# An encoder layer with a routed mixture of experts: the experts' token columns selected on TensorE instead of passing through DRAM, and the norms between the stages moved off GpSimd

## The chip, the core and the metric

One NeuronCore of a Trainium2 chip runs the whole program. The metric is the device time of one execution in microseconds (us). TensorE is called PE here, its weight load PEld, VectorE DVE, ScalarE ACT, GpSimd POOL and SyncE SP. PE's granted clock has two levels in the profile, 1.2 and 2.4 GHz (0.50 and 1.00).

## What is computed

One encoder layer on two requests of 256 tokens (512 tokens, width 1024, all fp32). The first part is a token mixer (a wide input projection, spatial gating, multi-scale pooling, an output projection). The part that matters here comes after it:

```
x = LN(alpha * x + gate1 * t) * ln1_g + ln1_b          # t: the mixer's output
h = LN(x) * (1 + scale2) + shift2                       # h2 in the kernel
# router: top-1 group of 4, then top-2 of the 8 experts in the group, per token
out[token] += weight * (silu(h @ w_gate[e]) * (h @ w_up[e])) @ w_down[e]   # 32 experts, hidden 512
y = LN(alpha * x + gate2 * out) * ln2_g + ln2_b
```

Each token goes to two experts, so 1024 rows are spread over 32 experts, 32 on the mean. An expert is worked in rounds of CAP = 64 rows; one that has more gets further rounds. With these inputs one expert has a further round.

## The kernel before, in words

Every engine's instructions stand in one written order, with semaphores between the engines. The program has three stages.

The mixer (span 0 to 439.5 us) ends with the projection by w_out: eight halves (4 tiles of 128 tokens, 2 halves of 512 columns), each 24 matmuls of 128x512. DVE multiplies a half by gate1 out of PSUM (L1644), POOL adds it to the residual (L583, `half_out`).

The transition makes x and h2 of each of the 4 tiles. DVE computes both norms with bn_stats and bn_aggr (L1638, L1656, L1661, L1667, L1674, L1710), ACT takes the roots (L1247, L1251), DVE inverts them with a Newton step of five small operations. h2 is then written chunk by chunk: `by_chunk` on ACT (L1255) reads `scaled` in steps of 8 elements and writes h2 as [token, 8 chunks, 128], POOL adds shift2 (L588, `shifted`). For the last tile DVE does both in two operations (L1728). PE transposes h2 of each tile (L876) and multiplies by the router's weights (L684, `wr`), tile after tile, with dummy transposes (`keep_clock`, L881) behind. DVE makes the routing decisions from the logits (L1751 to L1788). PE counts rows per expert with small bf16 matmuls. DVE makes each assignment's row number (`pos`, L1801) and POOL scatters h2's rows, sorted by expert, into the DRAM tensor `packed_x` with 8 indirect DMAs (L608). For the first expert alone the rows are selected on PE from h2, with one-hot columns `sel` as the stationary side and h2 as the moving side, and transposed (L1029 to L1035).

The expert stage (482.6 to 969.7 us) runs the experts one after another. The 6 MB of weights of one expert, gate_w, up_w and down_w, are loaded by SP into three sets of buffers, `next_expert`: gate and up for expert e when expert e-3's are read, down when expert e-3's is read. Ahead of them SP loads the expert's 64 rows from `packed_x` into `xrows` (`load_rows`, L426). On PE an expert is: 32 matmuls of 64 stationary and 512 moving columns for gate and up (two column halves of the array work side by side), 4 transposes of the next expert's rows (L926), 4 transposes of the hidden values (L942), 16 matmuls for down. DVE and ACT make the steps between: silu (L1297), the product (L1888), `x_t` of the next expert (L1849), the columns of hid (L1072), the gated output (L1906). POOL stores the output rows to DRAM (L615), and each token gathers its two rows at the end.

An fp32 matmul is two rows for PE in the trace (hi and lo), an fp32 transpose is one. In the listings the weight-load side of a form is what stands first (128*64 is 128 partitions and 64 stationary columns), the moving side second.

```
def x_transposes(rows, bank, s):              # L926, before: 4 transposes per expert
    for k in range(KC // 2):
        x = pe.transpose(bank[:, cols], rows[:, cols], ident)
def h_transposes(hd, bank, sm):               # L942, before and after: 4 per expert
    view = hd[:, :].rearrange("c (p f) -> c f p", f=FC)       # FC = 4: steps of 16 bytes
```

Of the kernel before, what the change touches and what calls it, by code (L numbers as in the profile page):

```python
# [5 lines left out]
D = 1024  # L6
REQ = 2
SEQ = 256
TOK = REQ * SEQ
KC = D // 128  # L10
TILES = TOK // 128
HALF = 64
# [27 lines left out]
def hybrid_encoder(nc, x_prompt, x_sample, c_prompt, c_sample, w_mod, b_mod, w_in, b_in, w_spatial,  # L40
# [7 lines left out]
    packed_x = nc.dram_tensor("packed_x", (ASSIGN + 8 * CAP, D), f32).ap()  # L48
    mod_rows_d = nc.dram_tensor("mod_rows_d", (2, REQ, 2, 512), f32).ap()
    shift2_d = nc.dram_tensor("shift2_d", (REQ, KC, 2, 64), f32).ap()  # L50
# [3 lines left out]
    with ctx:  # L54
# [38 lines left out]
        halves = [at(f"half{i}", [128, 512], f32, SLOT + (32 + 2 * i) * K) for i in range(3)]  # L93
        scaled = [at(f"scaled{i}", [128, D], f32, SLOT + (38 + 4 * i) * K) for i in range(2)]
        last_half = at("last_half", [128, 512], f32, SLOT + 46 * K)
        gate1_bc = at("gate1_bc", [128, D], f32, S0 + 9728 + 8192)
        shift2_bc = at("shift2_bc", [128, KC, 128], f32, 2 * SLOT + 40 * K)
# [6 lines left out]
        is_last = at("is_last", [128, 2, TILES, CAP], f32, 2 * SLOT + 40 * K)  # L104
        scaling = at("scaling", [128, 2, 2, 128], f32, 2 * SLOT + 40 * K)
        weighed = at("weighed", [128, 2, TILES, CAP], f32, 2 * SLOT + 42 * K)
# [23 lines left out]
        pos = at("pos", [128, 2, TILES], u32, S0 + 2464)  # L130
        pos_y = at("pos_y", [128, 2, TILES], u32, S0 + 2496)
        tab = at("tab", [1, 5, NEXP + 1], i32, S0 + 2528)
# [5 lines left out]
        rel_last = at("rel_last", [128, 2, TILES], f32, P0 + 288)  # L138
        slot_p = at("slot_p", [128, 1], f32, S0 + 3392)
        assert P0 + 320 + base <= nc.sbuf_usable_end  # L140
        gate2_half = [at(f"gate2_half{r}", [128, 512], f32, o) for r, o in enumerate((T0 + 6144, S0 + 7680))]
        slot_gate = at("slot_gate", [128, 512], f32, T0 + 10240)
        slot_gate_x = at("slot_gate_x", [128, 512], f32, T0 + 27648)
        n0_next = at("n0_next", [128, NEXP], f32, T0 + 25600)
        slots_last = at("slots_last", [128, CAP], f32, T0 + 25728)
# [14 lines left out]
        h2 = [at(f"h2_{i}", [128, KC, 128], f32, T0 + o) for i, o in enumerate((12288, 16384, 20480, 8192))]  # L160
# [6 lines left out]
        onehot = at("onehot", [128, 2, TILES, NEXP], f32, Q0 + 736)  # L167
# [8 lines left out]
        slots = at("slots", [128, CAP], f32, T0 + 2176)  # L176
        sel = at("sel", [128, 2, TILES, CAP], f32, T0 + 2432)
        before_m = at("before_m", [128, 4, 128], bf16, T0 + 512)
        request_m = at("request_m", [128, 2, 128], bf16, T0 + 5504)
        slot_tmp = at("slot_tmp", [128, 2, CAP], f32, T0 + 2432)  # L180
        assert Q0 + 3936 + base <= nc.sbuf_usable_end

        xrows = [at(f"xrows{i}", [128, 512], f32, T0 + 4096 * i) for i in range(3)]

        x_t = [at(f"x_t{i}", [128, KC, CAP], f32, T0 + o) for i, o in enumerate((29696, 14336, 16384))]
        sg = at("sg", [CAP, DE], f32, T0 + 18432)
        hid = at("hid", [CAP, DE], f32, T0 + 20480)
        hid_t = at("hid_t", [128, FC, CAP], f32, T0 + 22528)
        yout = [at(f"yout{i}", [128, 512], f32, o) for i, o in enumerate((T0 + 23552, S0 + 3584, S0 + 5632))]
        xrows_x = at("xrows_x", [128, 512], f32, T0 + 2048)  # L190
        x_first = at("x_first", [CAP, D], f32, T0 + 25600)
        x_t_x = at("x_t_x", [128, KC, CAP], f32, T0 + 12288)
        sg_x = at("sg_x", [CAP, DE], f32, T0 + 31744)
        hid_x = at("hid_x", [CAP, DE], f32, T0 + 33792)
        hid_t_x = at("hid_t_x", [128, FC, CAP], f32, T0 + 35840)
        yout_x = at("yout_x", [128, 512], f32, T0 + 36864)
# [29 lines left out]
        s_wr = sem("s_wr")  # L226
        s_ln2 = sem("s_ln2")
        s_zero = sem("s_zero")
        s_scat = sem("s_scat")
        s_out = sem("s_out")  # L230

        pe_pro = sem("pe_pro")
# [137 lines left out]
        def _(sp):  # L370
# [88 lines left out]
            for e in range(3):  # L459
                load_rows(e, offset(e))  # L460
# [1611 lines left out]
```

## Time and profile before

| what | value |
|---|---|
| time before, median of 3 runs | 1003.95 us (1002.37 to 1005.49) |
| the profiled execution | 1002.76 us, span 1001.2 us, so 1.6 us lie outside the span |
| PE busy | 874.3 us, 87% of the span |
| DVE, ACT, POOL busy | 379.3, 209.4, 141.8 us |
| DMA | 310.50 MB, mean 310 GB/s |
| mean granted PE clock | 0.957 |

The page cuts the span in 40 slices of 25 us. A digit is a busy share in tenths. The windows view gives the same for stretches that one chooses: busy time and count for each engine, then the mean granted clock, the share of the DMA engines and GB/s. The timeline lists instructions in order of time, runs of equal ones merged into one row with their count; its second number is then the time from the start of the first to the end of the last. In the views by tile a row gives shortest, median and longest duration in ns.

### The profile page before, as it was taken

To read this page: it belongs to the slowest core of one execution; us is meant where nothing else is said; L and a number is where in the kernel's file an instruction comes from. 1 tells how busy PE (TensorE), PEld (TensorE's weight loads), DVE (VectorE), ACT (ScalarE), POOL (GpSimd) and SP (SyncE) were. 2 spreads that over 40 slices of the span, in tenths; PEclk is the share of its full clock that TensorE was granted. 3 is DMA by queue.
4 is the path that set the end of the run, shared out by engine and by line. 5 is a ranking of instruction groups with operands and counts; after the bars stand their busy time and mean duration, and the time that the engine had idled before them with its cause. 6 is when DMAs were issued, how large, how long until landed. Compare 5 with 4: busy or idle time off the path is not lost.

```text
span 1001.2 us, 12712 instructions
## 1 busy us (share of the span) xinstructions
PE 874.3 (87%) x4001; PEld 502.7 (50%) x4002; DVE 379.3 (38%) x672; ACT 209.4 (21%) x302; POOL 141.8 (14%) x192
## 2 busy tenths in 40 slices
PE   3789999999999999969778888997868888887895
PEld 2457677888888887859323233332223233322231
DVE  4522443565343247896412222222122122212145
ACT  2321334441234244122300000000000000000024
POOL 2210267000001000340300000000000000000041
PEclk9799999999999999986999999999999999999998
DMA  9894653365647624449699999999999999999984
GB/s 366 325 299 172 218 206 138 115 236 187 236 181 192 206 86 149 146 158 426 224 419 424 426 426 428 427 426 427 427 428 427 427 427 425 431 425 429 422 337 133
DMA packets 52557, 310.50 MB, mean 310 GB/s; under 512 B 5058, under 2 KB 7202, under 8 KB 36898
## 3 DMA queue, kind: packets, MB, share of 16 engines
q1 hardware_dynamic: 41104, 272.64, 67.2%
q0 software_dynamic: 10800, 35.64, 10.4%
q10 hardware_dynamic: 610, 1.66, 0.6%
q8 instruction: 26, 0.43, 0.2%
q14 instruction: 17, 0.14, 0.0%
HBM read 284.46 MB, written 25.45 MB: 310 GB/s over the span
## 4 chain that ended last, share of the span: by engine, by line
PE 60%; DMA 22%; DVE 6%; issue 3%; SPq 3%; ACT 3%; POOL 1%; DVEq 0%; POOLq 0%; ACTq 0%
PE bank L684 58%; DMA up_w<-in_w_exp_up 18%; DMA modraw<-in_w_mod 2%; SPq L385 2%; PE bank L942 1%; DVE hid L1888 1%; ACT sg L1297 1%; DVE res L1661 1%; DMA y_first<-round_y,pos_y 1%; DMA packed_x<-h,pos 1%; ACT hid_t L1072 1%; PE bank L881 1%; PE bank L876 1%; POOL packed_x L608 1%; DMA round_y<-yout 0%
## 5 line engine op out<-in xcount | busy, mean ns | idle before, releaser
L684 PE MATMUL bank<-gate_w,x_t 128*64 128x512 f32 x512 | 234.2, 611 | 28.7 <-DMA up_w<-in_w_exp_up 20.6
L684 PE MATMUL bank<-up_w,x_t 128*64 128x512 f32 x512 | 234.3, 612 | 0.0
L684 PEld LDWEIGHTS bank<-gate_w,x_t 128*64 128x64 f32 x512 | 70.6, 141 | 183.4 <-issue 180.0
L684 PE MATMUL bank<-down_w,hid_t 128*64 128x512 f32 x496 | 121.7, 636 | 14.7 <-ACT hid_t L1072 14.7
L684 PE MATMUL bank<-h_hi,w_hi 128*128 128x512 f32 x320 | 126.5, 395 | 1.6 <-ACT h_hi L1106 1.6
L684 PE MATMUL bank<-h_hi,w_lo 128*128 128x512 f32 x320 | 126.3, 395 | 0.0
L684 PE MATMUL bank<-h_lo,w_hi 128*128 128x512 f32 x320 | 125.0, 398 | 0.0
L1888 DVE TENSOR_TENSOR hid<-bank,sg 64x512 f32<-64x512 f32 x31 | 21.5, 693 | 226.7 <-ACT sg L1297 226.7
L1437 DVE TENSOR_TENSOR w_lo<-raw,w_hi 128x1024 fp32r<-128x1024 f32 x56 | 68.6, 1227 | 78.6 <-ACT w_hi L1072 78.5
L1297 ACT ACTIVATE sg<-bank 64x512 f32<-64x512 f32 x31 | 18.3, 590 | 378.8 <-PE bank L684 378.8
L615 POOL DMA_DIRECT2D round_y<-yout x31 | 16.1, 519 | 423.3 <-issue 423.3
L684 PEld LDWEIGHTS bank<-down_w,hid_t 128*64 128x64 f32 x496 | 34.8, 144 | 78.6 <-issue 59.6
L684 PEld LDWEIGHTS bank<-h_lo,w_hi 128*128 128x128 f32 x320 | 60.3, 189 | 25.1 <-issue 11.6
L684 PEld LDWEIGHTS bank<-up_w,x_t 128*64 128x64 f32 x512 | 70.5, 141 | 0.0
L1072 ACT ACTIVATE w_hi<-raw 128x1024 fp32r<-128x1024 f32 x56 | 58.9, 1053 | 53.3 <-PE bank L684 51.6
L684 PEld LDWEIGHTS bank<-h_hi,w_hi 128*128 128x128 f32 x320 | 61.4, 192 | 14.2 <-ACT h_hi L1106 2.0
L684 PEld LDWEIGHTS bank<-h_hi,w_lo 128*128 128x128 f32 x320 | 61.1, 191 | 13.1
L1906 DVE TENSOR_TENSOR yout<-bank,slot_gate 128x512 f32<-128x512 f32 x32 | 22.1, 692 | 104.7 <-PE bank L684 100.8
L684 PE MATMUL bank<-a_lo,w_hi 128*128 128x512 f32 x128 | 49.9, 390 | 0.3 <-DVE w_lo L1437 0.3
L684 PE MATMUL bank<-a_hi,w_lo 128*128 128x512 f32 x128 | 49.8, 389 | 0.0
L684 PE MATMUL bank<-a_hi,w_hi 128*128 128x512 f32 x128 | 49.8, 389 | 0.0
L942 PE MATMUL bank<-cst,hid 64*128 64x64 f32 x124 | 20.5, 285 | 28.5 <-DVE hid L1888 28.5
(328 smaller groups left out, 1005.8 us busy)
## 6 DMA issues: line engine op xcount, KB each, us to landing
down_w<-in_w_exp_down SPq DMA_DIRECT2D x32, 2048.0 KB, 30.3
gate_w<-in_w_exp_gate SPq DMA_DIRECT2D x31, 2048.0 KB, 24.9
up_w<-in_w_exp_up SPq DMA_DIRECT2D x31, 2048.0 KB, 29.6
modraw<-in_w_mod SPq DMA_DIRECT2D x24, 1024.0 KB, 8.4
raw<-in_w_in SPq DMA_DIRECT2D x9, 2048.0 KB, 9.7
round_y<-zrow POOLq DMA_DIRECT2D x6, 2048.0 KB, 7.6
xrows<-packed_x SPq DMA_DIRECT2D x32, 256.0 KB, 20.9
raw<-in_w_branch_b SPq DMA_DIRECT2D x2, 2048.0 KB, 9.4
```

Source lines behind the costliest of these rows:

```text
L385: sp.dma_start(modraw0[m][:, :, :], mod_source(m)).then_inc(s_m0[m], 16)
L608: pool.indirect_dma_start(packed_x[0:ASSIGN, :], bass.IndirectOffsetOnAxis(pos[:, j, i:i + 1], 0), h2[i][:, :, :].rearrange("p k n -> p (k ...
L615: pool.dma_start(round_y[bass.ds(row, rows), 0:512], y[0:rows, :]).then_inc(done, 16)
L684: return pe.matmul(out, lhsT, rhs, start=start, stop=stop, skip_group_check=True)
L876: x = pe.transpose(MX[hb][:, 128 * k:128 * k + 128], h2[i][:, 4 * hb + k, :], ident)
L881: pe.transpose(MX[0][:, 0:128], ident, ident)
L942: x = pe.transpose(bank[:, CAP * fc:CAP * fc + CAP], view[:, fc, :], ident[0:CAP, 0:CAP])
L1072: return act.activation(out, in_, ACT.Copy, scale=scale)
L1297: act.activation(sgb[:, :], bank[0:CAP, :], ACT.Silu).then_inc(sm["silu"], 1)
L1437: dve.tensor_tensor(w_lo[par][:, :, :], raw[:, u % 2, :, 128 * (b % 4):128 * (b % 4) + 128], w_hi[par][:, :, :].bitcast(f32), ALU.subtract ...
L1888: dve.tensor_tensor(gated_hid[:, :], B[0][CAP:128, :], silu[:, :], ALU.mult).then_inc(m_sem["hid"], 1)
L1906: dve.tensor_tensor(yout[s][:, :], B[1][:, :], slot_gate[:, :], ALU.mult).then_inc(m_sem["yo"], 1)
```

## The change

- `packed_x`, its 8 scatters on POOL, and the loads of rows on SP are gone. `xrows` and its semaphores are gone with them.
- New function `selected` on PE: for each of the 8 chunks of the width, four matmuls, one per token tile, with 128 columns of h2 as the stationary side and 64 one-hot columns as the moving side, summed in PSUM. The result is x_t of an expert, without transposes. It replaces `x_transposes` in every expert: chunks 0 to 3 stand ahead of the hidden transposes, chunks 4 to 7 behind them. Further rounds and the first expert use it too.
- The one-hot columns of the next expert are made on DVE (`chosen_rows`, a comparison of 128x256) from `slot_of`, a table of each token's place in each expert.
- h2 stays in the plain layout [token, 1024]. A chunk is read from it in steps of 8 elements (32 bytes), by the transposes ahead of the router and by `selected`.
- The norms: the residual is added on DVE with a running sum in the same operation, ACT computes the squared deviation, DVE makes the inverse root in four small operations and both affine parts. POOL does nothing there.
- On PE all h2 transposes of tiles 0 to 2 stand ahead of the router's matmuls of tiles 0 to 2; the gate2 matmuls move ahead of `keep_clock`, which goes from 36 and 8 transposes to 20 and 4.

```diff
-            pool.wait_ge(pool_h2, TILES - 1)
-            for j in range(2):
-                for i in range(TILES):
-                    pool.indirect_dma_start(packed_x[0:ASSIGN, :], bass.IndirectOffsetOnAxis(pos[:, j, i:i + 1], 0),
-                                            h2[i][:, :, :].rearrange("p k n -> p (k n)"), None, ...).then_inc(s_scat, 16)
...
             def next_expert(e, s):
-                load_rows(s, offset(e))
                 load_gate_up(e, s)
...
-            def x_transposes(rows, bank, s):
-                for k in range(KC // 2):
-                    cols = slice(128 * k, 128 * k + 128)
-                    x = pe.transpose(bank[:, cols], rows[:, cols], ident)
+            def selected(chosen, bank, chunks):
+                for kc in chunks:
+                    for i in range(TILES):
+                        by_chunk = h2[i][:, :].rearrange("t (p k) -> t k p", k=KC)
+                        x = mm(bank[:, CAP * kc:CAP * kc + CAP], by_chunk[:, kc, :], chosen[:, i, :], start=(i == 0), stop=(i == TILES - 1))
+                return x
...
                 gate_up(x_t[s], s, B[0], m_sem, ...)
-                if not (last or opening):
-                    next_rows()
+                else:
+                    pe.wait_ge(m_sem["sl"], e + 2)
+                    selected(sel, B[2], range(0, KC // 2))
                 pe.wait_ge(m_sem["hid"], e + 1)
-                h_transposes(hid_x if opening else hid, B[3], m_sem)
+                h_transposes(sg_hid, B[3], m_sem)
+                if not last:
+                    selected(sel, B[2], range(KC // 2, KC)).then_inc(m_sem["xs"], 1)
                 pe.wait_ge(m_sem["ht"], e + 1)
...
-            for i in range(TILES):
-                h2_transposes(i)
-                for kc in range(KC): ...       # the router's matmuls
-            keep_clock(36)
+            h2_transposes(0, (B[4], B[5]))
+            pe.wait_ge(dve_gated, 6)
+            h2_transposes(1, (B[0], B[1]))
+            pe.wait_ge(dve_gated, 8)
+            h2_transposes(2, (B[2], B[3]))
+            logits(0)
+            logits(1)
+            logits(2)
+            pe.wait_ge(act_rt, 2)
+            h2_transposes(3, (B[4], B[5]))
+            logits(3)
+            ...                                # the gate2 matmuls
+            keep_clock(20)
...
+            def chosen_rows(out, column):
+                return dve.tensor_tensor(out[:, :, :], slots_by_tile(TILES), slot_of[:, column, :]..., ALU.is_equal)
...
             def gated_half(h):
-                dve.tensor_tensor(halves[h % 3][:, :], B[h % 4][:, :], gate1_bc[...], ALU.mult).then_inc(dve_gated, 1)
+                dve.tensor_tensor(part, B[h % 4][:, :], gate1_bc[...], ALU.mult).then_inc(dve_gated, 1)
+                ch.did(dve.scalar_tensor_tensor(out=row, in0=part, scalar=1.0, in1=row, op0=ALU.mult, op1=ALU.add,
+                                                accum_out=fin[:, h % 2, h // 2:h // 2 + 1]))
```

One expert on PE, before: the end of its gate and up, then the next expert's rows, the hidden transposes and down (the row of 64x512 is one fp32 matmul, x7 the seven others).

```order
L684 MATMUL bank<-up_w_53,x_t_196 64x512
L926 MATMUL bank<-cst,xrows_194 128x128 [waits e_x2]
L926 MATMUL bank<-cst,xrows_194 128x128 x3
L942 MATMUL bank<-cst,hid 128x64 [waits e_hid]
L942 MATMUL bank<-cst,hid 128x64 x3
L684 MATMUL bank<-down_w_56,hid_t 64x512 [waits e_yo,e_dn1,e_ht]
L684 MATMUL bank<-down_w_56,hid_t 64x512 x7
```

The same place now, from the last four selecting matmuls of the first block on (h_0 to h_3 are the four token tiles; 16 such matmuls stand ahead of the hidden transposes, the first of them with [waits e_sl], and 16 behind).

```order
L588 MATMUL bank<-sel,h_0_156 128x64
L588 MATMUL bank<-sel,h_1_157 128x64
L588 MATMUL bank<-sel,h_2_158 128x64
L588 MATMUL bank<-sel,h_3_159 128x64
L855 MATMUL bank<-cst,sg_hid 128x64 [waits e_hid]
L855 MATMUL bank<-cst,sg_hid 128x64 x3
L588 MATMUL bank<-sel,h_0_156 128x64
L588 MATMUL bank<-sel,h_1_157 128x64
L588 MATMUL bank<-sel,h_2_158 128x64
L588 MATMUL bank<-sel,h_3_159 128x64
```

What was four transposes that wait for a DMA (e_x2) is 32 matmuls in two blocks that wait for DVE's one-hot columns (e_sl); the hidden transposes stand between the blocks.

The last tile's norm on DVE, before: it begins with the statistics of the half that POOL has added, and ends (13 rows further, not shown) with the two L1728.

```order
L1638 BN_STATS st<-res 128x6 [waits pool_half,dve_scaled]
L1649 TENSOR_TENSOR last_half<-bank,gate_bc 128x512 [waits pe_out]
L1651 TENSOR_TENSOR res<-res,last_half 128x512 [waits dve_c]
L1638 BN_STATS st<-res 128x6 [waits dve_half]
L1656 BN_AGGR mv<-st 128x2 [waits dve_c]
L1657 TENSOR_SCALAR rs<-mv 128x1 [waits dve_c]
L1661 SCALAR_TENSOR_TENSOR res<-res,mv,ln_bc 128x1024
```

And now:

```order
L1522 TENSOR_TENSOR z_row_92<-bank,gate_bc 128x512 [waits pe_out]
L1525 SCALAR_TENSOR_TENSOR res,fin<-z_row_92,res 128x512 [waits dve_gated]
L1539 TENSOR_SCALAR fin<-fin 128x1 [waits dve_c]
L1541 SCALAR_TENSOR_TENSOR z_row_92<-res,fin,ln_bc 128x1024 [waits dve_mean]
L1531 TENSOR_SCALAR fin<-fin 128x1 [waits act_sq]
L1532 RECIPROCAL fin<-fin 128x1
L1533 TENSOR_SCALAR fin<-fin 128x1 [waits dve_c]
L1534 TENSOR_SCALAR fin<-fin 128x1 [waits dve_c]
L1543 SCALAR_TENSOR_TENSOR res,rs<-z_row_92,fin,ln_bc 128x1024 [waits dve_c]
L1545 TENSOR_SCALAR rs<-rs 128x1 [waits dve_c]
L1550 SCALAR_TENSOR_TENSOR z_row_92<-res,rs,scale_bc 128x1024 [waits dve_mean]
```

The statistics are gone from DVE; it waits for ACT's root (act_sq) in the middle of each norm, and for nothing of POOL.

## Rows read from the trace of the kernel before

**Rows 1.** Windows view by stage: busy per engine, clock, DMA share, GB/s.

```profile
core 0: us, PE busy (x) PEld busy (x) DVE busy (x) ACT busy (x) POOL busy (x), PEclk, DMA share, GB/s
439.50:482.60 43.10, 33.44 (x191) 28.31 (x189) 33.44 (x108) 11.45 (x20) 9.61 (x7) 0.68 0.92 380
482.60:969.70 487.10, 409.35 (x1849) 147.12 (x1850) 117.58 (x230) 38.84 (x71) 39.85 (x71) 0.96 0.99 414
```

**Rows 2.** Timeline, PE, one expert: start, time, what; idle time before in brackets.

```profile
587.58 0.59 PE L684 MATMUL bank<-gate_w,x_t 128*64 128x512 f32 x1
...
594.55 0.66 PE L926 MATMUL bank<-cst,xrows 128*128 128x128 f32 x4
596.13 0.66 PE L942 MATMUL bank<-cst,hid 64*128 64x64 f32 x4 [0.92 <-DVE hid L1888]
597.27 3.65 PE L684 MATMUL bank<-down_w,hid_t 128*64 128x512 f32 x16 [0.47 <-ACT hid_t L1072]
600.75 0.59 PE L684 MATMUL bank<-gate_w,x_t 128*64 128x512 f32 x1
```

**Rows 3.** Windows view, the router's stretch and that expert; columns as in Rows 1.

```profile
448.00:467.00 19.00, 18.73 (x87) 18.03 (x87) 12.86 (x37) 5.97 (x11) 2.16 (x1) 0.50 1.00 427
587.60:600.70 13.10, 11.70 (x58) 4.32 (x56) 3.22 (x5) 0.98 (x2) 0.99 (x2) 1.00 1.01 425
```

**Rows 4.** DMA issues: count, KB each, median us to landing.

```profile
xrows<-packed_x SPq DMA_DIRECT2D x32, 256.0 KB, 20.9
```

**Rows 5.** By tile, PE: ns shortest/median/longest; first and last start; form.

```profile
L942 PE MATMUL bank<-cst,hid x124: 280/280/302, 507.3 to 965.2; 64*128 64x64 f32 x124
L684 PE MATMUL bank<-wr,h_t x64: 407/408/429, 448.3 to 467.1; 128*128 128x36 f32 x64
L1035 PE MATMUL bank<-cst,x_first x8: 221/223/242, 481.1 to 481.6; 64*128 64x64 f32 x8
```

**Rows 6.** Groups by form, DVE and ACT: us in all, mean ns; idle before.

```profile
L1651 DVE TENSOR_TENSOR res<-res,last_half 128x512 f32<-128x512 f32 x1 | 0.7, 692 | 0.0
L1728 DVE SCALAR_TENSOR_TENSOR h<-scaled,rs,shift_bc 128x512 f32<-128x512 f32 x2 | 2.2, 1150 | 0.0
L1710 DVE SCALAR_TENSOR_TENSOR scaled<-res,mv,scale_bc 128x1024 f32<-128x1024 f32 x4 | 5.1, 1276 | 0.0
L1356 ACT ACTIVATE squares<-y_first,fin 128x1024 f32<-128x1024 f32 x4 | 4.6, 1146 | 2.2 <-DVE fin L1968 2.2
```

**Rows 7.** Timeline, PE, from the router to the first expert.

```profile
448.26 3.63 PE L684 MATMUL bank<-wr,h_t 128*128 128x36 f32 x16 [7.79 <-ACT h_t L1072]
...
467.34 5.65 PE L881 MATMUL bank<-cst 128*128 128x128 f32 x36
472.83 0.29 PE L684 MATMUL bank<-both,before_m 128*128 128x160 bf16 x2
...
481.13 0.68 PE L1035 MATMUL bank<-cst,x_first 64*128 64x64 f32 x8 [0.94 <-DVE x_first L1829]
482.59 0.61 PE L684 MATMUL bank<-gate_w,x_t 128*64 128x512 f32 x1 [0.78 <-ACT x_t L1072]
```

**Rows 8.** Timeline, DVE, the last tile's norm and the first routing step.

```profile
446.19 0.67 DVE L1649 TENSOR_TENSOR last_half<-bank,gate_bc 128x512 f32<-128x512 f32 x1
...
457.23 2.22 DVE L1728 SCALAR_TENSOR_TENSOR h<-scaled,rs,shift_bc 128x512 f32<-128x512 f32 x2
...
467.57 0.31 DVE L1751 TENSOR_TENSOR lg<-bank,br_bc 128x144 f32<-128x144 f32 x1 [5.74 <-PE bank L684]
```

**Rows 9.** Timeline, PE, the one further round, the last expert, what follows it.

```profile
779.64 0.63 PE L926 MATMUL bank<-cst,xrows_x 128*128 128x128 f32 x4
...
795.48 0.59 PE L684 MATMUL bank<-gate_w,x_t 128*64 128x512 f32 x1
...
956.31 0.59 PE L684 MATMUL bank<-gate_w,x_t 128*64 128x512 f32 x1
...
969.58 1.98 PE L684 MATMUL bank<-res,cst 128*128 128x512 f32 x4
```

More of the change, by code:

```diff
@@ L640, in further_rounds @@
                 with pool.If(more > 0):
[L641 to L645 removed]
+                    with pool.Fori(0, more) as r:
+                        store_further(r)
             def expert(e, s):
[L648 removed]
+                more, first = turns_of(e)
                 turn = pool.snap(first + e)
@@ L656, in expert @@
                     store(yout[s], turn, y_st[s], CAP)
-                further_rounds(e, off, more, first)
+                further_rounds(e, more, first)
             with pool.Fori(0, 10) as t:
@@ new lines, in _ @@
+            for i in range(TILES - 1):
+                deviation1(i)
+                deviation2(i)
+            deviation1(3)
+            for hb in range(2):
+                h2_columns(0, hb, (B[4], B[5]))
+            for hb in range(2):
+                h2_columns(1, hb, (B[0], B[1]))
+            deviation2(3)
+            for hb in range(2):
+                h2_columns(2, hb, (B[2], B[3]))
+            h2_columns(3, 0, (B[4], B[5]))
+            act.wait_ge(pe_lg, TILES + 1)
+            copy(gate2_half[0][:, :], B[5][:, :])
@@ L1670, in variance2 @@
-            def variance2(i, biased):
-                dve.wait_ge(dve_c, biased)
-                for hb in range(2):
-                    read = ch.did(dve.bn_stats(st[:, i, hb, :], res[:, i, 512 * hb:512 * hb + 512]))
-                dve.wait_ge(dve_c, read)
-                aggregated = ch.did(dve.bn_aggr(mv2[:, i, :], st[:, i, :, :].rearrange("p a b -> p (a b)")))
-                dve.wait_ge(dve_c, aggregated)
-                dve.tensor_scalar(rs[:, 5, i:i + 1], mv2[:, i, 1:2], EPS, None, ALU.add).then_inc(dve_st, 1)
@@ L1907, in expert @@
+                if not last:
+                    dve.wait_ge(m_sem["xs"], e + 2)
+                    rows_in(x_t[(s + 1) % 3], B[2]).then_inc(m_sem["xt"], 1)
+                    if not (isinstance(e, int) and e == NEXP - 2):
+                        chosen_rows(sel, s + 2).then_inc(m_sem["sl"], 1)
+                dve.wait_ge(m_sem["ym"], e + 1)
+                dve.tensor_tensor(yout[s][:, :], B[1][:, :], yout[s][:, :], ALU.mult).then_inc(m_sem["yo"], 1)
                 further_rounds(s, *(turns or turns_of(e)))
```

595 lines of the change are left out of this document (204 added, 391 removed).

## Prediction

> **What bounds the kernel now.** I read the windows view by stage first, since the share of busy time hides that the stages have different limits. The expert stage is 487.1 us of the 1001.2, its DMA engines are busy to 0.99 at 414 GB/s, and PE to 409 of 487 us [rows 1]. So the loads bound it, with PE close behind. How close is seen in the timeline of an expert that waited for no load: the next gate matmul starts 600.75 - 587.58 = 13.17 us after this one's, with the DMA engines full at 425 GB/s and the clock at 1.00 [rows 2, 3]. An expert's 6.29 MB of weights take 14.8 us at 425 GB/s; the rows that SP loads add 0.26 MB, 0.6 us [rows 4]. The stage's mean is 487/33 = 14.8 us a round (32 experts and one further round). PE has thus only 1.5 to 2 us of slack in an expert. Whatever lengthens PE's expert past about 15 us is paid in full, 31 times.
>
> **Price of a selecting matmul.** The change puts 32 fp32 matmuls into each expert, 64 rows of PE, each with 128 stationary columns of h2 and 64 moving ones. No row of before has exactly this. Three are near. The hidden transposes have 128 stationary columns read in steps (16 bytes) and 64 moving: four rows take 0.66 us, one is 0.28 long, so they start (0.66 - 0.28) / 3 = 0.127 us apart, the first step being the longest; about 0.12 in the run [rows 2, 5]. The router's matmuls are real fp32 ones with a contiguous 128-column stationary side and only 36 moving columns: 16 rows in 3.63 us, one 0.408 long, (3.63 - 0.41) / 15 = 0.215 us apart at the lower clock [rows 5, 7], which is 0.107 at the upper one. With 36 columns the moving side can't be what takes that long, so it is the weight load. The transposes of x_first, contiguous with 64 moving, start (0.68 - 0.22) / 7 = 0.065 us apart [rows 5, 7], but a transpose is one row and no real fp32 matmul. I take 0.12: the hidden transposes share the stepped read, the 64 moving columns and the clock. The bounds are 0.107 below and, since h2 is now read in steps of 32 bytes where the transposes have 16, more above: DVE's two reads in steps of 32 bytes take 1150 ns for 512 elements where a plain one takes 692 [rows 6], some 1.9 ns an element once a fixed 0.16 us is taken off. At 1.9 ns each, 128 columns would take 0.25 us.
>
> The Trainium skill's page "TensorE: Matmul & The Clock Gate", section "LDWEIGHTS (loading the stationary operand)", gives a weight load as its columns divided by 1.2, in ns, so 107 for 128; by that price the 64 rows would be 6.8 us and the sum below 1096. The page "SBUF — State Buffer", section "Door 1: The DMA port swizzle", says that SBUF has 16-byte cachelines and each access that crosses to a new one pays a penalty. The stepped transposes (0.12) against the contiguous ones (0.065) agree with it; that it can cost more at 32 bytes than at 16 no row shows.
>
> **An expert on PE after.** From 13.17 us I take out the piece from the row transposes to the hidden transposes, 596.13 - 594.55 = 1.58, and the one from there to down, 597.27 - 596.13 = 1.14 [rows 2]; both hold the waits for DVE (0.92) and ACT (0.47). In their place come 32 rows of selection, 3.84 us, four hidden transposes, 0.48, and 32 rows more, 3.84. The first block hides the wait for hid, the second the wait for hid_t: that is the one gain. 13.17 - 1.58 - 1.14 + 3.84 + 0.48 + 3.84 = **18.61 us**. That is above the loads' 15, so PE becomes the bound, the loads run ahead, and what the change saves in DMA (8 MB of rows, the scatter) buys nothing. On DVE an expert adds only a comparison of 128x256 and a copy behind the second block, and down's 3.4 us cover them.
>
> **The transition.** Before, DVE lags: the w_out matmuls end at 439.4, but the last half is taken up at 446.19 and h2 ends at 457.23 + 2.22 = 459.45 [rows 8]. After, a tile costs DVE four half operations (0.69 each), four full ones (1.28), ten small ones (0.17) and two waits of about 0.5 for ACT's square and root (1.15 + 0.5 against DVE's 1.28) [rows 6]: 10.6 us, against 10.9 that PE takes for a tile. So it keeps pace, and the last h2 is there about 10 us after the last matmul, at 449.3. PE: tiles 0 to 2 of the router run from about 444 on, each 3.43 us at the lower clock (I expect it to fall again, as it did from 443 on), then the last tile's transposes and matmuls, to 458.3; before, the logits were there at 467.57 [rows 8]. The routing steps from there to the counts stay 5.3 us (472.83 - 467.57), the gate2 matmuls and 20 dummies fit into them within 0.4. From the counts to the first gate matmul it was 9.76 us [rows 7]. It will be 0.75 for the counts, 0.9 for slot_of and the comparison, 7.7 for 64 rows, 1.0 for signals and the copy: 10.4. So the first gate matmul starts at 458.3 + 5.7 + 10.4, about **474.5, 8 us earlier**. Where the scatter and the first rows' loads held back expert 1, nothing does now.
>
> **Sum.** 474.5 + 31 x 18.61 (576.9) + the further round + the last expert + the tail. The further round was 795.48 - 779.64 = 15.8 us [rows 9]. It begins with 64 rows that nothing hides, 7.7 us instead of 0.6, and a wait for DVE's columns, 1: about 24. The last expert has no selection: 969.58 - 956.31 = 13.3 [rows 9]. Tail 1001.2 - 969.6 = 31.6, same operations. Total 474.5 + 576.9 + 24 + 13.3 + 31.6 = 1120.3 of span, with 1.6 outside **1122 us**, against 1002.8 for the profiled execution. That one lies 1.2 under the median, so I leave it at 1122.
>
> **Rivals.**
> *A. As above* (the load of 128 stepped columns takes 0.107 to 0.125 us, clock stays up). 0.107 gives 6.8 us of selection, 17.8 an expert, 1122 - 26 = 1096; four us of doubt in the transition make the low end 1090.
> *B. The clock falls in the selection,* or a row takes 0.13 to 0.19. For it: in 448 to 467 PE was busy 18.73 of 19.00 us with the router's matmuls and transposes, and the granted clock was 0.50 throughout [rows 3]. Selection now takes 8.2 us in one stretch. Against: in the normal expert the clock is 1.00 though 1.4 of 13.1 us are idle. Price: if it falls in every expert, part of the second block runs at 0.215 instead of 0.12 (+3), and the first part of down or gate at half rate (+3.4): 25 us an expert, 1122 + 31 x 6.4 = 1320.
> *C. The 32-byte step costs the full 0.25 us.* 64 rows are 16 us, an expert 26.8, and the clock falls too: 1380 to 1500. For it the DVE rows, against it that PE reads 16-byte steps in half that time per element, through a read path of its own. A mechanism of memory would hit both.
> *D. Selection at 0.065, faster than before.* If the second row of a pair needs no load of its own, or the load hides, 64 rows take 4.1 us, the expert 15.0, under what the loads need without the rows (15.2). Then loads bound the stage as before, less 29 x 0.6 = 17.8 us at most, and the transition gives 10: 975 to 1000, say 985. It decides at 0.07 us a row. Against: the router's 64 rows for 32 matmuls each have their load [rows 3, 5], at 256 cycles each by their spacing.
>
> The Trainium skill's page on TensorE, section "Architectural detail", says a matmul can begin before its weight load ends; were the load hidden by this, D would hold. The router's rows speak against it.
>
> **How the numbers follow.** A 0.60, B 0.20, C 0.12, D 0.08. The range takes A and B, 1090 to 1325, and leaves out 0.20. A difference under 0.3% (3 us) can't be told from none: of D's 0.08 I give 0.06 to faster and 0.02 to the same, the rest, 0.92, is slower.
>
> **What would show it.** In the trace after: the selecting matmuls' spacing (0.12, not 0.065, 0.2), 32 rows on each side of the hidden transposes without idle time; 18.6 us from gate to gate; no wait for up_w in the stage; DMA share down from 0.99 to about 0.8 (6.4 MB in 18.6 us is 345 GB/s); granted clock above 0.95 in the stage; first gate matmul near 474.5. The prediction is wrong if the spacing is off, since 0.01 us a row moves it by 20 us, or if the clock in the stage is well under 1.

## The result and the profile after

The changed kernel takes 1446.62 us (median of 4 runs, 1445.89 to 1450.98), the kernel before 1004.13 us beside it (1002.37 to 1005.49). The ratio is 1.4417, 95% interval 1.438 to 1.4454. The direction was right, the size was far off: 1446.6 lies outside the range of 1090 to 1325 and inside what rival C gave (1380 to 1500). The profiled execution has a span of 1443.8 us and a mean granted clock of 0.813.

From the page of after: busy time, the clock's row of the 40 slices (36 us each), and the costliest groups (busy us, mean ns, idle before).

```profile
PE 1395.2 (97%) x5941; PEld 995.6 (69%) x5942; DVE 379.7 (26%) x699; ACT 211.6 (15%) x313; POOL 113.6 (8%) x174
PEclk9899999999997678767776776777668767776788
L588 PE MATMUL bank<-sel,h 128*128 128x64 f32 x2048 | 503.5, 432 | 0.3 <-DVE sel L1635 0.3
L588 PE MATMUL bank<-down_w,hid_t 128*64 128x512 f32 x512 | 169.6, 822 | 0.5 <-ACT hid_t L965 0.5
```

The selection (31 experts' and the first one's) is 2048 rows, 503.5 us of PE, and waits for 0.3 us in all. In the expert stage the clock is at 6 to 8 tenths. The windows view of the expert stage (columns as in [rows 1]):

```profile
481.80:1412.20 930.40, 923.59 (x3769) 633.05 (x3769) 131.16 (x273) 38.85 (x71) 38.39 (x69) 0.74 0.53 205
```

The stage takes 930.4 us where it took 487.1 [rows 1], its DMA share is 0.53 instead of 0.99, and PE is busy for 923.6 of it. So PE is the bound, as predicted, only by much more. One expert in the timeline (PE; start, time, what), which answers to [rows 2]; its first gate matmul starts at 711.29, the next expert's at 739.57:

```profile
718.25 7.87 PE L588 MATMUL bank<-sel,h 128*128 128x64 f32 x32
726.06 0.74 PE L855 MATMUL bank<-cst,sg_hid 64*128 64x64 f32 x4
726.73 7.87 PE L588 MATMUL bank<-sel,h 128*128 128x64 f32 x32
734.52 5.21 PE L588 MATMUL bank<-down_w,hid_t 128*64 128x512 f32 x16
```

32 rows take 7.81 us from start to start of what follows: 0.244 us a row over the block (7.87 less the last row's own length of 0.43, over 31, is 0.240). I had 0.12. Behind the second block down takes 5.2 us where it took 3.65 [rows 2]. The expert is 28.28 us, and PE waits for nothing in it. The transition in the timeline of PE, which answers to [rows 7]:

```profile
439.32 2.84 PE L776 MATMUL bank<-cst,h 128*128 128x128 f32 x24
443.33 3.76 PE L588 MATMUL bank<-wr,h_t 128*128 128x36 f32 x32 [1.18 <-ACT h_t L965]
...
463.71 0.45 PE L588 MATMUL bank<-both,before_m 128*128 128x160 bf16 x2
...
465.51 15.49 PE L588 MATMUL bank<-sel,h 128*128 128x64 f32 x64 [0.30 <-DVE sel L1635]
481.78 1.09 PE L588 MATMUL bank<-gate_w,x_t 128*64 128x512 f32 x1 [0.78 <-ACT x_t L965]
```

The logits are there at about 455.8 (458.3 was said), the counts start at 463.7 against 472.83 in [rows 7]. The 64 selecting rows then take 15.5 us instead of 7.7, and the first gate matmul comes at 481.78, no earlier to speak of than before.

The question was thus what makes a selecting row cost 0.24 us, and what of the 443 us is the row's price and what the clock. Theory: the read of the stationary side in steps. Rivals: a real fp32 matmul of this shape costs that however it is read; or the price follows the length of the step, as rival C had it.

### The profile page after: what moved, and what is told of

It reads as the page before. It is cut to its first block, busy times and chain, and to the rows that moved or that the text cites. A ratio compares the mean times of both kernels' runs of the same rounds, so it can differ in the third digit from the quotient of the medians.

```text
span 1443.8 us, 15921 instructions
## 1 busy us (share of the span) xinstructions
PE 1395.2 (97%) x5941; PEld 995.6 (69%) x5942; DVE 379.7 (26%) x699; ACT 211.6 (15%) x313; POOL 113.6 (8%) x174
## 4 chain that ended last, share of the span: by engine, by line
PE 89%; DMA 4%; DVE 2%; SPq 1%; ACT 1%; issue 1%; POOL 0%; DVEq 0%; POOLq 0%; ACTq 0%
PE bank L588 87%; PE bank L855 1%; DMA modraw<-in_w_mod 1%; SPq L366 1%; DMA shift_bc<-mod_rows_d 1%; DMA y_first<-round_y,pos_y 1%; PE bank L790 0%; DVE res L1543 0%; DVE h L1552 0%; ACT squares L1139 0%; DVE z_row L1550 0%; DVE res L1525 0%; DVE z_row L1522 0%; PE bank L645 0%; DMA round_y<-yout 0%
## 5 line engine op out<-in xcount | busy, mean ns | idle before, releaser
L588 PEld LDWEIGHTS bank<-sel,h 128*128 128x128 f32 x2048 | 491.8, 334 | 29.2 <-issue 25.2
L588 PE MATMUL bank<-sel,h 128*128 128x64 f32 x2048 | 503.5, 432 | 0.3 <-DVE sel L1635 0.3
L588 PE MATMUL bank<-gate_w,x_t 128*64 128x512 f32 x512 | 226.6, 596 | 0.8 <-ACT x_t L965 0.8
L588 PE MATMUL bank<-up_w,x_t 128*64 128x512 f32 x512 | 226.6, 596 | 0.0
L588 PE MATMUL bank<-down_w,hid_t 128*64 128x512 f32 x512 | 169.6, 822 | 0.5 <-ACT hid_t L965 0.5
L1682 DVE COPY x_t<-bank 128x512 f32<-128x512 f32 x31 | 21.4, 692 | 420.0 <-PE bank L588 420.0
L588 PEld LDWEIGHTS bank<-down_w,hid_t 128*64 128x64 f32 x512 | 46.2, 190 | 99.4 <-issue 95.3
L1182 ACT ACTIVATE sg_hid<-bank 64x512 f32<-64x512 f32 x32 | 18.9, 590 | 601.2 <-PE bank L588 601.2
L1722 DVE TENSOR_TENSOR sg_hid<-bank,sg_hid 64x512 f32<-64x512 f32 x32 | 22.2, 695 | 199.4 <-ACT sg_hid L1182 199.4
L1741 DVE TENSOR_TENSOR yout<-bank,yout 128x512 f32<-128x512 f32 x32 | 22.1, 692 | 136.3 <-PE bank L588 136.3
```

Of the source, the lines that this page charges most:

```text
L588: return pe.matmul(out, lhsT, rhs, start=start, stop=stop, skip_group_check=True)
L1182: act.activation(sgb[0:CAP, :], bank[0:CAP, :], ACT.Silu).then_inc(sm["silu"], 1)
L1682: return dve.tensor_copy(xt[:, :, :].rearrange("p k c -> p (k c)"), bank[:, :])
L1722: dve.tensor_tensor(sg_hid[CAP:128, :], B[0][CAP:128, :], sg_hid[0:CAP, :], ALU.mult).then_inc(m_sem["hid"], 1)
L1741: dve.tensor_tensor(yout[s][:, :], B[1][:, :], yout[s][:, :], ALU.mult).then_inc(m_sem["yo"], 1)
```

## Experiments

**The step of the read: packed and step16.** In packed only the layout of h2 is changed: VectorE writes it so that each chunk lies contiguous, and the transposes ahead of the router and the selection read it so. In step16 a chunk is read in steps of 16 bytes instead of 32.

```diff
-                dve.scalar_tensor_tensor(out=h2[i][:, :], in0=z, ...
+                dve.scalar_tensor_tensor(out=h2[i][:, :].rearrange("t (k p) -> t p k", k=KC), in0=z.rearrange("t (p k) -> t p k", k=KC), ...
...
-                        by_chunk = h2[i][:, :].rearrange("t (p k) -> t k p", k=KC)
+                        by_chunk = h2[i][:, :].rearrange("t (k p) -> t k p", k=KC)          # packed
+                        by_chunk = h2[i][:, :].rearrange("t (h p k) -> t h k p", h=2, k=4)  # step16
```

> Edit: h2 is written by VectorE chunk after chunk, so that `selected` and the transposes read their 128 columns contiguously; nothing else changes. Theory 1 (the step of the stationary read is what costs): rows of the selecting matmuls drop from 0.238 us to about 0.107 at the upper clock, an expert to about 17.9 us, the time to 1100 to 1120 us. Theory 2 (a real fp32 matmul with 128 stationary and 64 moving columns costs 0.238 however it is read): no change, 1447 us. Theory 3 (step and clock): once the load is contiguous it goes with the clock, and if the clock falls in the selection rows take 0.107 to 0.213 us, 1150 to 1300 us.

> Edit: h2 is laid out so that a chunk is read in steps of 4 elements (16 bytes) instead of 8 (32 bytes). If the price goes with the length of the step, a row costs about 0.12 us and the time comes to 1120 to 1300 us. If any step that leaves no two columns in one 16-byte piece costs the same, a row stays at 0.238 and the time at 1440 to 1450 us.

packed took 1132.81 us (4 runs, 1131.47 to 1136.9), ratio to before 1.1307 (1.1269 to 1.1344); theory 1 had said 1100 to 1120, with 0.107 a row and 17.9 an expert. step16 took 1437.96 us (one run), 2 us under what a flat price gave. One expert of packed in the timeline; its gate starts at 702.22, the next at 720.72, so 18.5 us:

```profile
709.18 3.79 PE L588 MATMUL bank<-sel,h 128*128 128x64 f32 x32
712.90 0.69 PE L855 MATMUL bank<-cst,sg_hid 64*128 64x64 f32 x4
713.52 3.79 PE L588 MATMUL bank<-sel,h 128*128 128x64 f32 x32
717.23 3.65 PE L588 MATMUL bank<-down_w,hid_t 128*64 128x512 f32 x16
```

And the stage of packed in the windows view, mean clock 0.99:

```profile
476.90:1080.00 603.10, 596.41 (x3687) 362.29 (x3688) 125.88 (x262) 35.80 (x66) 31.95 (x62) 0.99 0.81 314
```

A block of step16:

```profile
716.64 7.73 PE L588 MATMUL bank<-sel,h 128*128 128x64 f32 x32
```

So the step is the cause: same instructions, same shapes, and a block takes 3.79 us contiguous (3.72 to the next start, 0.116 a row) and 7.87 stepped. The rival that a real matmul of this shape costs it anyhow is out. And the price doesn't follow the step's length: at half the step a block takes 7.73. One more thing went with it that I hadn't foreseen: with the contiguous read the clock stays at the upper level in the experts, and down is back at 3.65. (It falls in the further round, whose 64 rows take 11.4 us at a mean clock of 0.62.)

**The disputed price by itself: steps_bench and bench2.** The kernel before, with series of 24 instructions on PE behind its last result, plain contiguous transposes between the series. The edit, for one series:

```diff
+            def columns(step, n=128):
+                return flat[:, 0:step * n].rearrange("p (c k) -> p k c", k=step)[:, 0, :]
+            for _ in range(24):
+                mm(B[1][:, 0:64], columns(8), ident[:, 0:64])
```

> The kernel before, with series of 24 matmuls or transposes on PE behind its last result, each series with its own read step of the stationary side (4, 8, 16, 32, 64, 128 bytes) and 24 contiguous transposes between. If the step's length sets the price, real fp32 rows go 0.107, 0.107, 0.12, 0.24, 0.48, 0.96 us. If only leaving the 16-byte piece does, 0.107, then about 0.24 from 16 bytes on and flat. If the moving side matters, the series with 32 or 128 moving columns differ from the one with 64. Transposes in the same steps: twice the contiguous price (0.06 to 0.12) and flat, or growing with the step.

> The kernel before with a second set of series behind its last result. Real fp32 matmuls with the stationary side in steps of 3, 6 and 8 elements (12, 24, 32 bytes): if two columns in one 16-byte piece are what makes it cheap, 12 bytes lies between 0.117 and 0.235 us, 24 bytes is 0.235. Transposes of 64 rows (64 moving columns) with 128 stationary columns in steps of 1, 3, 4, 8 elements: 0.065 contiguous and 0.12 from 16 bytes on, that is also a factor of two. Real matmuls with the 32-byte step and 256 and 512 moving columns: 0.235 for 256 if the load runs beside the moving of the row before, and 0.235 for 512 too (512 columns alone take 0.22).

Timeline, PE, steps_bench: the series with steps of 4, 8, 16, 32 and 64 bytes, then 32 bytes with 32 and with 128 moving columns, then 64 stationary columns in steps of 32 bytes, then the step on the moving side.

```profile
1008.57 5.47 PE L684 MATMUL bank<-cst,res 128*128 128x64 f32 x48
1016.50 5.76 PE L684 MATMUL bank<-cst,res 128*128 128x64 f32 x48
1024.73 11.35 PE L684 MATMUL bank<-cst,res 128*128 128x64 f32 x48
1039.48 11.59 PE L684 MATMUL bank<-cst,res 128*128 128x64 f32 x48
1055.49 10.61 PE L684 MATMUL bank<-cst,res 128*128 128x64 f32 x48
1083.83 11.52 PE L684 MATMUL bank<-cst,res 128*128 128x32 f32 x48
1099.84 11.57 PE L684 MATMUL bank<-cst,res 128*128 128x128 f32 x48
1113.96 5.97 PE L684 MATMUL bank<-cst,res 128*64 128x64 f32 x48
1122.54 5.82 PE L684 MATMUL bank<-res,cst 128*128 128x64 f32 x48
```

From the start of a series to the start of what follows, over 48 rows, a row costs 0.110 us contiguous, 0.117 at 8 bytes, 0.232 at 16, 0.237 at 32, 0.217 at 64, 0.216 at 128. bench2 adds 24 bytes, 0.222 (1026.60 to 1037.27, 48 rows), and 12 bytes, 0.184 (1009.32 to 1018.13). The last is a mean over both levels of the clock. The windows view (PE alone: busy, granted clock, DMA share, GB/s) has

```profile
1009.32:1015.20 5.88, 5.88 (x37) 1.00 0.00 0
1015.20:1018.10 2.90, 2.90 (x15) 0.50 0.00 0
```

and by the starts of the single rows they stand 0.173 us apart in the first stretch and 0.213 in the second. The price goes with the stationary columns (64 of them: 0.123) and not with the moving ones (32, 64 and 128: 0.236 to 0.238). A step on the moving side costs next to nothing (0.1175).

bench2, the transposes of 64 rows with 128 stationary columns in steps of 4, 16 and 32 bytes (12 bytes, not shown, is like 16), and then real matmuls with the 32-byte step and 512 and 256 moving columns:

```profile
1064.44 1.73 PE L1089 MATMUL bank<-cst,res 64*128 64x64 f32 x24
...
1082.40 3.09 PE L1095 MATMUL bank<-cst,res 64*128 64x64 f32 x24
1092.12 2.89 PE L1098 MATMUL bank<-cst,res 64*128 64x64 f32 x24
1101.55 20.89 PE L684 MATMUL bank<-res 128*128 128x512 f32 x48
1128.82 11.79 PE L684 MATMUL bank<-res 128*128 128x256 f32 x48
```

A transpose costs 0.069 contiguous and 0.118 to 0.126 stepped: a factor of 1.7 to 1.8. A real row goes from 0.110 to 0.237: a factor of 2.1. That is where my price went wrong: I took over the stepped transposes' 0.12 as it stood, where only their ratio to the contiguous ones could be carried over. With 256 moving columns a row still costs 0.242, so the load runs beside the moving of the row before it. With 512 it costs 0.432, which I had put at 0.235; I had read the 0.22 of gate and up as the price of 512 columns, but those are two matmuls side by side on the two column halves, each half with a row every 0.43 us (in after gate_w's rows start at 711.29, 711.72, 712.15).

The same series tell of the clock. Windows view of steps_bench, PE alone: the series at 4 bytes, at 32 bytes with 64 moving columns, and the same with 128 moving columns:

```profile
1008.60:1013.80 5.20, 5.20 (x50) 1.00 0.00 0
1039.50:1050.80 11.30, 11.30 (x50) 0.73 0.01 1
1099.90:1111.20 11.30, 11.30 (x49) 1.00 0.00 0
```

All three are fully busy in the listing. The second and the third have the same price per row, 11.39 and 11.41 us for 48 rows from start to start, at a mean clock of 0.73 and of 1.00. So the price of the stepped load doesn't go with PE's clock. The two blocks of one expert in after show the same, 7.81 and 7.79 us:

```profile
718.20:726.00 7.80, 7.80 (x34) 0.88 0.91 350
726.80:734.50 7.70, 7.70 (x32) 0.50 0.43 185
```

Contiguous rows do go with the clock. In no_sel (below), whose h2 is packed, the same 64 rows stand ahead of the first expert and in the further round:

```profile
471.20:478.50 7.30, 7.30 (x64) 1.00 0.86 364
760.60:774.40 13.80, 13.80 (x64) 0.50 1.01 429
```

7.4 and 13.9 us, 0.115 and 0.217 a row; the router's rows had 0.215 at the lower level [rows 5, 7]. So at the lower clock the step costs little (15.5 us for 64 rows in after, 13.9 here), and at the upper one it doubles the price. The fall of the clock in the experts comes with the stepped read, since packed differs from after by the layout of h2; what in the slow loads brings it about these runs don't show.

**Is it so much a row: half_sel.** The selection of chunks 4 to 7 is left out in the 31 experts, so the kernel computes with stale columns there.

```diff
-                if not last:
-                    selected(sel, B[2], range(KC // 2, KC)).then_inc(m_sem["xs"], 1)
```

> The changed kernel with half the selection left out: chunks 0 to 3 only in each of the 31 experts, chunks 4 to 7 of x_t are stale. If the price is so much a row and nothing else, 31 x 7.87 = 244 us less: 1200 to 1205 us. If the selection also costs through the clock that it pulls down in down's matmuls (4.7 to 6.2 us instead of 3.65), half of it lets the clock stay up and the time falls further, to 1150 to 1170 us.

1236.05 us (one run), above both expectations: less was gained than the block that is gone. Timeline of one expert:

```profile
707.11 7.89 PE L588 MATMUL bank<-sel,h 128*128 128x64 f32 x32
...
716.15 5.58 PE L588 MATMUL bank<-down_w,hid_t 128*64 128x512 f32 x16 [0.47 <-ACT hid_t L963]
```

The time fell by 210.6 us, 6.8 an expert. The block that is gone was 7.79 from start to start; the wait for hid_t that it had covered is back (16.9 us in all, 0.5 an expert), and the clock did not come back with half the selection: down takes 5.6 us here, and is busy for 184.2 us in all against 169.6 in after, 0.5 an expert more. So the cost of the clock is not in proportion to the selection.

**The other way round, and no selection at all: swap and no_sel.** In swap h2 is packed and the sides change places: the one-hot columns are loaded (64), h2 moves (512 columns), two halves side by side; then a copy and four transposes as before.

```diff
-                        x = mm(bank[:, CAP * kc:CAP * kc + CAP], by_chunk[:, kc, :], chosen[:, i, :], ...)
+                    for c in range(2):
+                        x = mm(bank[CAP * c:CAP * c + CAP, :], chosen[:, i, :], h2[i][:, 512 * c:512 * c + 512], ...)
...
+                    x_transposes(xrow, B[2], m_sem, e + 2)
```

> Edit: the sides are swapped and h2 is packed: 8 matmuls per expert with the one-hot columns as the stationary side (128x64) and h2 as the moving side (512), two column halves side by side, then a copy and four transposes of 128x128 as before. If PE goes by the rows of the profile (16 matmuls of 64x512 in 3.65 us, so 1.85 for 8; four transposes 0.66) an expert is 13.8 us on PE, the loads bound the stage again without the rows through DRAM, and the time is 975 to 994 us, say 982. If the waits for hid and the copies are not hidden, PE needs 15.0 us an expert and the time is about 996. If the selection on PE is costly in any form, above 1050.

> The packed version with the selection left out of the 31 experts (they multiply the first expert's columns; the further round still selects), so no rows through DRAM and none on TensorE. It gives what a selection at no cost would be worth. If the loads of 6.29 MB per expert bound the stage, the 0.6 us of rows per expert are saved and the first gate is at about 477: 975 to 985 us. If something other than the bytes sets 14.8 us an expert, about 997. TensorE's expert is 13.2 us when it waits for no load.

swap took 1022.77 us (4 runs, 1018.7 to 1024.23), ratio 1.019 (1.0154 to 1.0226): 110 us better than packed, but still behind the kernel before, and not the 982 that I expected. Timeline of one expert, from the gate at 626.92 to the next at 642.26, so 15.34 us:

```profile
633.79 3.60 PE L590 MATMUL bank<-h,sel 128*64 128x512 f32 x16
637.32 0.69 PE L863 MATMUL bank<-cst,sg_hid 64*128 64x64 f32 x4
638.19 0.66 PE L847 MATMUL bank<-cst,xrow 128*128 128x128 f32 x4 [0.17 <-DVE xrow L1746]
638.77 3.65 PE L590 MATMUL bank<-down_w,hid_t 128*64 128x512 f32 x16
```

The eight matmuls are 16 rows and take 3.5 us, not 1.85. I had taken [rows 2]'s "x16" for 16 matmuls, but it counts rows; down is eight matmuls. With that, PE needs 15.3 us an expert, waits for no weights in the stage, and stays the bound by a little. The description of the kernel before has the same slip: gate and up are 16 matmuls (32 rows) and down is 8 (16 rows).

no_sel, 989.33 us (one run), shows what a selection at no cost in the 31 experts would be worth: some 15 us. Its stage in the windows view, and in it the stretch of the further round, which still selects:

```profile
479.30:942.30 463.00, 389.28 (x1728) 149.39 (x1729) 126.74 (x264) 35.83 (x66) 31.94 (x62) 0.94 0.96 408
758.00:790.00 32.00, 26.61 (x106) 17.84 (x108) 4.16 (x10) 0.97 (x2) 1.07 (x2) 0.64 0.71 292
```

From the gate ahead of the further round to the next it is 48.03 us where an expert is 13.2 to 14.8, so the further round is about 34: its 64 rows take 13.9 us at the lower clock behind a wait of 2.6, and the DMA share falls to 0.71. The 31 experts are then (463.0 - 34) / 31 = 13.8 us each, where before they were (956.31 - 482.59 - 16) / 31 = 14.8 [rows 7, 9]. So 1.0 us an expert was saved, more than the 0.6 of the rows, and the further round took some 18 us of it back. That is why it isn't the 975 to 985 that I expected, and 15 us is no ceiling for a design whose further round is cheaper.

**The transition alone: norms_only, early_load, select_two.** norms_only is the kernel before with only the change's norms, residual and transposes ahead of the router; the rows still pass through DRAM. One place of it:

```diff
-                pool.tensor_tensor(part, part, halves[h % 3][:, :], ALU.add).then_inc(pool_half, 1)
+                ch.did(dve.scalar_tensor_tensor(out=row, in0=part, scalar=1.0, in1=row, op0=ALU.mult, op1=ALU.add,
+                                                accum_out=fin[:, h % 2, h // 2:h // 2 + 1]))
```

> Only the transition's part of the change, on the kernel before: norms on VectorE and ScalarE, residual with a running sum, the new order of the transposes ahead of the router, h2 written chunk after chunk; rows still pass through DRAM and no expert selects but the first. Theory: the logits are there at about 456 instead of 467.6 and, the expert stage being bound by loads that start as its buffers come free, all of it passes on: 992 to 996 us, ratio about 0.99. Rival: the rows' way through DRAM or the weights' loads end last ahead of expert 1, and nothing is gained, 1001 to 1003 us.

1000.34 us (5 runs, 998.22 to 1000.75), ratio 0.9958 (0.9943 to 0.9973): 0.4% faster than the kernel before, some 4 us where the theory said 8 to 12. Timeline of PE, the first gate matmul, the rows of expert 1 and its gate:

```profile
474.09 0.61 PE L658 MATMUL bank<-gate_w,x_t 128*64 128x512 f32 x1 [0.78 <-ACT x_t L1053]
493.62 0.65 PE L908 MATMUL bank<-cst,xrows 128*128 128x128 f32 x4 [4.46 <-DMA xrows<-packed_x]
495.70 1.09 PE L658 MATMUL bank<-gate_w,x_t 128*64 128x512 f32 x1 [1.44 <-DVE x_t L1783]
```

The first expert starts 8.5 us earlier than in [rows 7]. Expert 1 then waits for its rows out of DRAM. In the kernel before its gate started at 498.67, so 3 of the 8.5 us are left there; the timeline of before:

```profile
498.67 0.61 PE L684 MATMUL bank<-gate_w,x_t 128*64 128x512 f32 x1 [1.45 <-DVE x_t L1849]
```
The windows view of norms_only shows a DMA share of 0.65 in 480 to 500 us, in a stage that is bound by loads. Two attempts to fill that gap:

```diff
+                    load_gate_up(e, s)          # early_load: expert 3's weights ahead of the first rows
+                    first_rows()
                     load_rows(s, offset(e))
```

> norms_only with one more edit: SyncE issues gate_w and up_w of expert 3 as soon as expert 0's gate and up are read, ahead of its wait for the scatter and of the first experts' rows; in norms_only they are issued at 495.65 us though their buffers are free at 481, and the DMA engines are nearly idle from 486 to 496. Theory (the loads bound the expert stage, so idle time of the DMA engines there is lost for good): expert 1 starts about 3 us later, since its rows now queue behind 4 MB, but the stage ends up to 7 us earlier, 992 to 996 us. Rival (the start of expert 1 is what counts): 1002 to 1004 us, slower than norms_only.

select_two does this too, and gives expert 1 its rows on PE from h2, with swap's eight matmuls:

```diff
+                if opening:
+                    pe.wait_ge(dve_one, 1)
...
+                            x = mm(B[2][CAP * c:CAP * c + CAP, :], sel[:, 0, i, :], h2[i][:, 4 * c:4 * c + 4, :]..., ...)
```

> norms_only with expert 1's rows selected on TensorE from h2 too (8 matmuls with one-hot columns as the stationary side, as the first expert's, a copy, four transposes), so that its start waits for no rows from DRAM, and with expert 3's weights issued ahead of the rows' loads. If the way of the rows through DRAM ahead of expert 1 is what kept half of the transition's gain, expert 1's gate starts at about 489 us instead of 495.7, the DMA engines' idle time from 486 to 496 shrinks, and the time is 992 to 996 us. Rival: the scatter still ends last (expert 1's silu and output wait for it, and it is slowed by the weights' loads as in early_load, ending near 498), so that expert 1 only waits at another place: 1000 to 1004 us.

early_load: 1005.44 us (12 runs, 995.87 to 1007.41), ratio 1.0011 (0.9992 to 1.0029). select_two: 1002.77 us (12 runs, 999.97 to 1004.7), ratio 0.9994 (0.9981 to 1.0008). Neither is told from the kernel before, and norms_only's gain is gone in both. From the view of PE's waits of early_load (us in all, times, longest), and from the timeline and the windows view of select_two:

```profile
PE bank L915 <- DMA xrows<-packed_x: 14.1, 1, 14.1
```

```profile
505.08 1.09 PE L919 MATMUL bank<-cst,xrows 128*128 128x128 f32 x4 [8.07 <-DMA xrows<-packed_x]
480.00:500.00 20.00, 16.66 (x80) 6.06 (x76) 2.08 (x3) 0.97 (x2) 0.00 (x0) 1.00 1.02 430
500.00:520.00 20.00, 14.45 (x58) 5.30 (x59) 5.39 (x10) 1.11 (x3) 2.20 (x4) 0.74 0.53 176
```

The gap in the DMA only moved: full to 500 us, then 0.53. The scatter of h2 is what got slower beside the weights that are issued early: it starts at about the same time (its first DMA at 467.1 in early_load, 467.9 in norms_only), but the slowest of its eight DMAs lands 21.2 us after its issue, where it was 11.4, and SP, which waits for it, issues the first rows at 498.2 instead of 489.3. The transposes that wait for the rows start at 502.4 instead of 493.6. In select_two expert 1 starts its gate at 489.97, as the theory had it, and the wait comes at expert 2's rows (issued at 502.3, transposes at 505.1). The next gate and up wait behind that. The rival held in both. So the start of the stage hangs on the scatter and the first rows, and norms_only is the best version that I have.

## Why the prediction was wrong

- **What bounds the kernel.** Right. PE became the bound, there is no wait for up_w in the stage, and the DMA share fell (0.53; 0.81 in packed, where I had said 0.8).
- **Price of a selecting row, the failed step.** Taken 0.12, measured 0.24. I compared with the stepped transposes and argued from shape, clock and step. But with the same 32-byte step a transpose costs 0.12 and a real row 0.24, and a transpose's contiguous price (0.069) is well under a real row's (0.110). The partitions (64 there, 128 here) don't explain it: steps_bench's stepped transposes with 128 partitions and 128 moving columns cost 0.111 to 0.120. What is roughly alike is the factor between stepped and contiguous (1.7 to 1.8 and 2.1), not the price. Both contiguous prices stood in my own rows (0.065 and 0.107): 0.107 x 0.12 / 0.065 = 0.20 was to be had before the run, 5 us an expert more than I said. By my own estimate that would have moved the forecast to about 1290, two thirds of the way in the row's price; it would still have missed the result, since the factor isn't quite the same and the clock's part in down isn't in it. The argument against rival C, "PE reads 16-byte steps in half that time per element", rests on the same mistake.
- **Rival C.** Its time held, its mechanism by half. The price is near the 0.25 that it took over from DVE; a common cause in memory would fit, but no run tests it, and the price doesn't grow with the step: 0.232 at 16 bytes, 0.237 at 32, 0.217 at 64. I gave it 0.12, and with that the range ended at 1325. The Trainium skill's page "SBUF — State Buffer", section "Door 1: The DMA port swizzle", has 16-byte cachelines and a penalty for each access that crosses to a new one; the series agree with a rise up to there and none beyond (0.117 at 8 bytes, 0.173 at 12, 0.232 at 16, 0.237 at 32). Its page "TensorE: Matmul & The Clock Gate", section "LDWEIGHTS (loading the stationary operand)", gives 107 ns for 128 columns; that agrees with the contiguous series alone (0.110), and the stepped load is twice it.
- **An expert.** 18.61 predicted. With the contiguous read, at 0.116 a row, packed shows 18.5: everything but the price was right, the hidden waits included. In after the mean is (1398.84 - 481.78 - 34.2) / 31 = 28.5 us, the 34.2 being the further round. Of the 9.9 too little, 7.9 are the two blocks (15.6 for 7.7), 0.2 the hidden transposes (0.67 for 0.48), and 1.6 down at the lower clock (4.7 to 6.2 us an expert; busy 169.6 us in all against 118.6 in packed).
- **The clock.** Rival B's question was answered the other way round: with contiguous selection, as busy as it is, the clock is 0.99 in the stage, with the stepped one 0.74. The fall costs little inside the selection, whose stepped rows don't go with the clock, and 51 us in all in down.
- **The transition.** Right up to the counts: last h2 at 448.9 (449.3 said), logits at 455.8 (458.3), counts at 463.7 (463.9). The first gate matmul was 7.3 late (481.8 for 474.5), all of it the 64 rows (15.5 for 7.7). What I had not seen is that with rows through DRAM more than half of such a gain is lost again at expert 1 (8.5 us early, then 3).
- **Further round and tail.** 34.2 instead of 24: the 64 rows again (+7.8), and the wait for DVE's columns, 2.6 instead of 1. Last expert 13.3 and tail 31.6 as said.
- **The sum.** 31 x 9.87 = 306, + 10 + 7 = 323 of the 325 us between prediction and result. packed against after gives it by measurement: 1446.6 - 1132.8 = 314 us hang on the step of one read, and only 11 us lie between packed and the 1122 that I predicted. The 314 are 31 x 8.17 = 253 for the two blocks (7.81 + 7.79 against 3.72 + 3.71), 51 for down and 2 for the hidden transposes at the lower clock, 8 for the first expert's 64 rows (15.5 against 7.4), and 4 for the further round's (15.5 against 11.4, the clock having fallen there in packed too): 318, less 3 that packed's longer writes of h2 lose ahead of the first expert.

## What to carry to other kernels

When a price is taken from a neighbouring operation, carry over the ratio between two of its forms and apply it to the base price of the operation in question, as a better guess and not as a bound: here it gave 0.20 where 0.24 was measured and 0.12 had been said. A few series of 24 instructions behind the last result, as in steps_bench, would have measured it. Give the stationary side of a real fp32 matmul a contiguous view and put the step on the moving side or in the write that makes the operand: here four writes that are 0.8 us longer each (2048 ns against 1284) save 314 us. It does not make the change pay: packed is still 13% slower than before, since even contiguous rows put 7.4 us into an expert in which PE had 1.5 to 2 us of slack. And look what a gap in the DMA stands beside: here bulk loads put into it ran beside the scatter that the stage's start hangs on, and delayed just that.

## What the runs showed of the hardware

- Real fp32 rows with 128 stationary columns and 64 moving stand 0.110 us apart with a contiguous stationary side at the upper clock, 0.117 in steps of 8 bytes, 0.173 of 12, 0.232 of 16, 0.222 of 24, 0.237 of 32, 0.217 of 64, 0.216 of 128 (steps_bench, bench2); with 64 stationary columns 0.123 at 32 bytes.
- At the lower clock contiguous rows stand 0.217 apart (no_sel) and rows in steps of 12 bytes 0.213; in steps of 32 bytes they cost the same at both levels (7.81 and 7.79 us a block in after, at 0.88 and 0.50).
- Transposes go from 0.069 to 0.12 (64 moving columns); with 128 moving columns little of it is seen (0.109 contiguous, 0.111 to 0.120 stepped).
- The stepped load hides behind the moving side of the row before: 0.242 with 256 moving columns, 0.432 with 512, where gate_w's rows of 512 columns also start 0.43 apart. A step of 32 bytes on the moving side costs 0.007.
- The mean clock was 0.73 in fully busy series of 48 rows at 32 bytes with 32 or 64 moving columns, and 1.00 with 128 moving columns, with 64 stationary columns, and in the contiguous series.
- VectorE's write of h2 in steps of 512 bytes took 2048 ns for 1024 elements, the plain one 1284. In two halves that write in runs of 16 bytes (step16) it was 749 ns a half.
- The slowest of eight scatters of h2's rows landed 21.2 us after its issue with 4 MB of weights issued beside them (early_load), 11.4 us without (norms_only).
